# A two-block fp32 network on one core: the second block's layers without a loop, last granules in two row passes

## What is computed

```python
h = jnp.einsum('bsd,dc->bsc', x, w_in)
qa, ka, va, za, qb, kb, vb, zb, f_logit, g_logit = jnp.split(h, SPLIT_POINTS, axis=-1)
out_a = dilated_mixture(rope(qa), rope(ka), va)
up_a = jnp.einsum('bsw,wd->bsd', out_a * jax.nn.silu(za), w_up_a)
out_b = forgetting_attention(qb, kb, vb, log_f)
up_b = jnp.einsum('bsw,wd->bsd', out_b * jax.nn.silu(zb), w_up_b)
gates = jax.nn.sigmoid(g_logit + b_gate)
y = jnp.einsum('bsd,de->bse', g_a * up_a + g_b * up_b, w_out)
return layer_norm(DEEPNORM_ALPHA * x + y, ln_g, ln_b)
```

## Time and profile before

| what | value |
|---|---|
| median of 3 executions | 2982.62 us (2982.52 to 2982.68) |
| the profiled execution, its own time | 2983.63 us |
| span of the profiled execution | 2981.8 us |
| PE busy | 2835.0 us (95%) |
| DVE busy | 1838.4 us (62%) |
| ACT busy | 1352.2 us (45%) |
| DMA, 16 engines, share of the span | 58.3% for the hardware queue, 604 MB in all |
| first layer of the second block begins on PE | at 972.5 us of the span |
| first layer's last matmul ends | at 1961.2 us |
| second layer's last matmul ends | at 2964.9 us |

### The profile page before, as it was taken

One profiled execution on the slowest core, in us unless ns is written; L12 is line 12 of the kernel. 1 busy time (PEld: TensorE's weight loads), 2 busy tenths in 40 slices (PEclk: granted clock), 3 DMA queues, 4 the chain that ended last, 5 costly groups with the idle time before them and its releaser, 6 DMA issues.

```text
span 2981.8 us, 37910 instructions
## 1 busy us (share of the span) xinstructions
PE 2835.0 (95%) x13440; PEld 2346.0 (79%) x13440; DVE 1838.4 (62%) x2049; ACT 1352.2 (45%) x1741; POOL 64.0 (2%) x86
## 2 busy tenths in 40 slices
PE   1799999899999999999999999989999999999997
PEld 1578887688887788888888888868888888888886
DVE  8888988767854655555455455565655554545565
ACT  1244554444644444444454544434445445445443
POOL 0400000000000000000000000000000000000000
PEclk9899999899999999999999999989999999999999
DMA  9787678667545555556555565645554655555664
GB/s 372 279 303 267 237 249 327 215 227 231 171 142 169 192 173 171 176 198 201 188 172 173 177 190 186 228 135 176 176 177 160 229 191 176 176 177 174 194 212 141
DMA packets 165357, 604.32 MB, mean 203 GB/s; under 512 B 19192, under 2 KB 19360, under 8 KB 163904
## 3 DMA queue, kind: packets, MB, share of 16 engines
q1 hardware_dynamic: 160336, 583.08, 58.3%
q0 software_dynamic: 4848, 18.91, 2.1%
HBM read 599.79 MB, written 2.12 MB: 202 GB/s over the span
## 4 chain that ended last, share of the span: by engine, by line
PE 66%; DVE 1%; issue 1%; DMA 0%; ACT 0%; DVEq 0%; ACTq 0%; SPq 0%
PE acc L729 61%; PE psT L656 2%; PE psS L689 1%; PE psS L679 1%; PE psT L662 1%; PE psS L696 0%; DVE x L605 0%; DMA raw<-in_w 0%; DVE x L616 0%; DVE x L609 0%; ACT whi L304 0%; DVE wlo L408 0%; DVE stage L440 0%; DVE x L580 0%; DVE x L618 0%
## 5 line engine op out<-in xcount | busy, mean ns | idle before, releaser
L408 DVE TENSOR_TENSOR wlo<-raw,whi 128x1024 fp32r<-128x1024 f32 x672 | 822.7, 1225 | 863.6 <-ACT whi L304 860.5
L304 ACT ACTIVATE whi<-raw 128x1024 fp32r<-128x1024 f32 x672 | 711.6, 1060 | 991.4 <-PE acc L729 979.0
L729 PE MATMUL acc<-whi,xhi 128*128 128x512 f32 x2304 | 637.1, 398 | 9.9 <-DVE xlo L414 9.1
L729 PE MATMUL acc<-whi,xlo 128*128 128x512 f32 x2304 | 618.7, 390 | 0.0
L729 PE MATMUL acc<-wlo,xhi 128*128 128x512 f32 x2304 | 617.6, 390 | 0.0
L729 PEld LDWEIGHTS acc<-whi,xlo 128*128 128x128 f32 x2304 | 433.7, 188 | 92.5
L729 PEld LDWEIGHTS acc<-wlo,xhi 128*128 128x128 f32 x2304 | 433.0, 188 | 91.5
L729 PEld LDWEIGHTS acc<-whi,xhi 128*128 128x128 f32 x2304 | 423.5, 189 | 90.8 <-issue 9.5
L1245 ACT ACTIVATE whi<-raw 128x1024 fp32r<-128x1024 f32 x240 | 253.2, 1058 | 380.7 <-PE acc L1972 243.8
L1430 DVE TENSOR_TENSOR wlo<-raw,whi 128x1024 fp32r<-128x1024 f32 x232 | 283.0, 1223 | 163.2 <-ACT whi L1245 162.0
L1972 PE MATMUL acc<-whi,hhi 128*128 128x512 f32 x960 | 278.3, 412 | 13.6 <-DVE hlo L1441 8.3
(11 more groups left out here) (291 smaller groups left out, 1944.1 us busy)
## 6 DMA issues: line engine op xcount, KB each, us to landing
raw<-in_w SPq DMA_DIRECT2D x912, 512.0 KB, 3.5
mraw<-in_w_mod SPq DMA_DIRECT2D x150, 512.0 KB, 4.2
scr<-in_w_mod SPq DMA_DIRECT2D x31, 512.0 KB, 6.3
b_stage<-in_w_mod SPq DMA_DIRECT2D x11, 512.0 KB, 6.2
gate_row<-in_bg POOLq DMA_DIRECT2D x16, 256.0 KB, 5.2
gb<-cum_rows POOLq DMA_DIRECT2D x2, 1536.0 KB, 8.8
x<-in_x SPq DMA_DIRECT2D x1, 2048.0 KB, 8.2
gain<-in_g_post POOLq DMA_DIRECT2D x2, 1024.0 KB, 6.5
```

The lines of the kernel that those rows point to most:

```text
L304: act.activation(whi[:, n % SLOTS, :], raw[:, n % SLOTS, :], ACT.Copy).then_inc(s_hi, 1)
L408: dve.tensor_tensor(wlo[:, n % SLOTS, :], raw[:, n % SLOTS, :], whi[:, n % SLOTS, :].bitcast(F32), ALU.subtract).then_inc(s_lo, 1)
L729: m = pe.matmul(acc[c % 2][:, tb, :], a[:, kk, tile], b[:, n % SLOTS, k * CW:(k + 1) * CW], start=(kk == 0 and q == 0), stop=(kk == GK * g ...
```

## The change

**No loop.** PE, ACT and DVE have both layers written out one behind the other, and their waits compare with constants. SP's loop over the weights stays.

**The last granules** (`closing`). In the first layer the last 2 granules, in the second the last 4, run all their matmuls for row tile 0 first and then all for row tile 1. `s_half` comes at the end of row tile 0's, and `s_used` for these granules comes only in the row tile 1 pass.

**The first granules** of a layer (`leading`). The first two granules run row tile 0 for both and then row tile 1 for both. The first two fills change their shape: ("x", 0) is columns 0 to 511 of row tile 0 and ("x", 1) the same columns of row tile 1, so each holds what two granules need of one row tile.

**Between the layers** (`turn` on DVE). ACT and DVE split the next layer's first two weight granules before the residual. Then DVE carries row tile 0 through residual, statistics, deviation and the first 512 columns of the norm alone, takes up row tile 1's residual, splits fill ("x", 0), and so on. Gain and bias of columns 1024 to 2047 (`gained`) move behind the splits of granules 2 to 5 of the next layer's first chunk, in pieces of 256 columns of both row tiles.

**At the end** (`ending`). Row tile 0 is normalised while row tile 1 is still multiplied. The output goes out in five transfers by rows: 1024 and 1024 columns of row tile 0, then 1024, 512 and 512 columns of row tile 1.

The core of the diff:

```diff
+LEAD = 2
+CLOSING = (2, SLOTS)
+PIECES = ((0, 0, 2 * CW), (0, 2 * CW, 2 * CW), (1, 0, 2 * CW), (1, 2 * CW, CW), (1, 3 * CW, CW))
...
-        with act.Fori(0, DEPTH) as l:
+        for l in range(DEPTH):
...
+            if l < DEPTH - 1:
+                for g in range(LEAD):
+                    hi(g, l + 1)
+            for tb in range(TB):
+                standard_deviation(tb)
+                standardise(tb)
+                if l < DEPTH - 1:
+                    fill_hi(("x", tb), l + 1)
+            if l < DEPTH - 1:
+                hi(LEAD, l + 1)
...
+            def turn():
+
+                for g in range(LEAD):
+                    lo(g, l + 1)
+                last_residual(0)
+                variance(0)
+                inverse_deviation(0)
+                normalised(0, 0, CW).then_inc(s_xn, 1)
+                last_residual(1)
+                fill_lo(("x", 0), l + 1)
+                variance(1)
+                inverse_deviation(1)
+                normalised(1, 0, CW).then_inc(s_xn, 1)
+                link(normalised(0, CW, CW))
+                fill_lo(("x", 1), l + 1)
+                normalised(1, CW, CW).then_inc(s_xn, 2)
+                lo(LEAD, l + 1)
+
+            def ending():
+
+                last_residual(0)
+                variance(0)
+                inverse_deviation(0)
+                normalised(0, 0, 2 * CW).then_inc(s_fin, 1)
+                last_residual(1)
+                variance(1)
+                gained_rows(0, 2 * CW, 2 * CW).then_inc(s_fin, 1)
+                inverse_deviation(1)
+                normalised(1, 0, 2 * CW).then_inc(s_fin, 1)
+                gained_rows(1, 2 * CW, CW).then_inc(s_fin, 1)
+                gained_rows(1, 3 * CW, CW).then_inc(s_fin, 1)
...
+                    if c == 0 and l and g in range(LEAD, LEAD + 2 * (NCW - NV2)):
+
+                        gained(NV2 * CW + (g - LEAD) * CW // 2, CW // 2, l - 1).then_inc(s_xnp, 1)
...
+            def leading():
+
+                fill(("x", 0))
+                if l == 0:
+                    fill(("x", 1))
+                pe.wait_ge(*copied(l, ("x", 0)))
+                pe.wait_ge(s_acc[0], at(l, nch // 2, 1))
+                for g in range(LEAD):
+                    one_row(0, g, 0)
+                    if g == 0 and l:
+                        fill(("x", 1))
+                pe.wait_ge(*copied(l, ("x", 1)))
+                for g in range(LEAD):
+                    one_row(0, g, 1).then_inc(s_used, 1)
+                    if g == 0:
+                        fill(("x", 2))
+
+            def closing():
+
+                c = nch - 1
+                last = range(granules2(c) - CLOSING[l], granules2(c))
+                for tb in range(TB):
+                    for g in last:
+                        m = one_row(c, g, tb)
+                        if tb == 1:
+                            m.then_inc(s_used, 1)
+                        elif g == last[-1]:
+                            m.then_inc(s_half, 1)
```

More of the change, by code:

```diff
@@ L396, in _ @@
         links = [0]
-        with dve.Fori(0, DEPTH) as l:
+        for l in range(DEPTH):
             def link(ins):
@@ L588, in _ @@
-            link(last)
             dve.wait_ge(s_lnp, at(l, 32, 32))
             dve.memset(rtmp[:, 0:1], 0.0)
-            for tb in range(TB):
-                last = dve.bn_aggr(mv[:, tb, :], stats[:, tb, :, :])
-            last.then_inc(s_var, 1)
-            dve.wait_ge(s_std, l + 1)
-            link(dve.reciprocal(rstd[:], std[:]))
-            dve.scalar_tensor_tensor(out=nmr[:], in0=mv[:, :, 0], scalar=-1.0, in1=rstd[:], op0=ALU.mult, op1=ALU.mult)\
-                .then_inc(s_rstd, 1)
@@ L620, in _ @@
-        assert links[0] == VLINKS2, links
+            if l < DEPTH - 1:
+                turn()
+            else:
+                ending()
     @block.tensor
@@ L624, in _ @@
         pe.wait_ge(s_mem, 2)
-        with pe.Fori(0, DEPTH) as l:
+        for l in range(DEPTH):
             def fill(name):
@@ L698, in unit, with accumulate @@
                 m.then_inc(s_sfull, 1)
+            def accumulate(c, g, order):
+                ahead, alow = (ahi, alo) if CHUNKS2[c][0] == "u" else (xhi, xlo)
+                products = ((ahead, whi), (alow, whi), (ahead, wlo))
+                n = FIRST2[c] + g
+                for q, k, tb in order:
+                    a, b = products[q]
+                    kk = GK * g + k
+                    m = pe.matmul(acc[c % 2][:, tb, :], a[:, kk, tb * P:(tb + 1) * P],
+                                  b[:, n % SLOTS, k * CW:(k + 1) * CW], start=(kk == 0 and q == 0),
+                                  stop=(kk == GK * granules2(c) - 1 and q == 2))
+                return m
@@ new lines, in high, with low, one_row @@
+            def high(n):
+                pe.wait_ge(s_hi, at(l, GRAN2, n + 1))
+            def low(n):
+                pe.wait_ge(s_lo, at(l, GRAN2, n + 1))
+            def one_row(c, g, tb):
+                n = FIRST2[c] + g
+                if tb == 0:
+                    high(n)
+                accumulate(c, g, [(q, k, tb) for q in (0, 1) for k in range(GK)])
+                if tb == 0:
+                    low(n)
+                return accumulate(c, g, [(2, k, tb) for k in range(GK)])
@@ L700, in _ @@
+            def closing():
+                c = nch - 1
+                last = range(granules2(c) - CLOSING[l], granules2(c))
+                for tb in range(TB):
+                    for g in last:
[4 more added lines that the diff above has]
+                            m.then_inc(s_half, 1)
+            leading()
             for c, (kind, j) in enumerate(CHUNKS2):
-                ahead, alow = (ahi, alo) if kind == "u" else (xhi, xlo)
@@ L702, in _ @@
-                for g in range(granules2(c)):
+                for g in range(LEAD if c == 0 else 0, granules2(c) - (CLOSING[l] if c == nch - 1 else 0)):
                     for name in fills2(c, g):
@@ L716, in _ @@
                     n = FIRST2[c] + g
-                    pe.wait_ge(s_hi, at(l, GRAN2, n + 1))
-                    products = ((ahead, whi), (alow, whi), (ahead, wlo))
-                    steps = [(q, k, tb) for q in (0, 1) for k in range(GK) for tb in range(TB)]
-                    steps += [(2, k, tb) for k in range(GK) for tb in range(TB)]
-                    if n == GRAN2 - 1:
-                        steps = [(q, k, tb) for tb in range(TB) for q in range(3) for k in range(GK)]
-                    for i, (q, k, tb) in enumerate(steps):
-                        if q == 2 and all(p < 2 for p, _, _ in steps[:i]):
-                            pe.wait_ge(s_lo, at(l, GRAN2, n + 1))
-                        a, b = products[q]
-                        tile = slice(tb * P, (tb + 1) * P)
-                        kk = GK * g + k
-                        m = pe.matmul(acc[c % 2][:, tb, :], a[:, kk, tile], b[:, n % SLOTS, k * CW:(k + 1) * CW],
-                                      start=(kk == 0 and q == 0),
-                                      stop=(kk == GK * granules2(c) - 1 and q == 2))
-                        if n == GRAN2 - 1 and (q, k, tb) == (2, GK - 1, 0):
-                            m.then_inc(s_half, 1)
-                    m.then_inc(s_used, 1)
+                    high(n)
+                    accumulate(c, g, [(q, k, tb) for q in (0, 1) for k in range(GK) for tb in range(TB)])
+                    low(n)
+                    accumulate(c, g, [(2, k, tb) for k in range(GK) for tb in range(TB)]).then_inc(s_used, 1)
+            closing()
 def rope_tables():
```

157 lines of the change are left out of this document (85 added, 72 removed).

## The result

The changed kernel takes 2965.47 us (median of 6 runs, 2963.08 to 2968.32), the kernel before beside it 2982.65 us (6 runs, 2981.19 to 2984.9). The ratio is 0.9941 with a 95% interval of 0.9928 to 0.9954: faster by 17.2 us. The forecast was 2970.0 with a range of 2967.0 to 2973.0. So the direction was right, and the gain was larger than the range allowed.

What follows compares the result with a forecast made beforehand. PE, busy throughout inside the layers, was taken as the bound, leaving two seams to win: the turn between layers 8.5 us and the end 4.2, together 12.7; 2982.62 - 12.7 = 2969.9, stated as 2970.0, range 2967.0 to 2973.0.

Steps and rivals of the forecast that it cites:

- the name of a row: Between the layers: the ninth granule began at 2001.74 before, 40.6 us after the last matmul, and would begin at 1991.9.
- The clock: Behind the pause between layers: falls to half speed for about 4.4 us, net cost about 1.3 us, ends 0 and 2.5.
- Rival 1: Between the layers: the clock stays up, so the turn gives 9.8 us and the time is 2968.6; chance 0.27.
- the chosen case: Between the layers: the clock falls, the turn gives 8.5 us and the time is 2969 to 2971; chance 0.43.
- Constants in place of registers: In the waits: gives nothing, since PE is always busy; at most 0.8 us.
- The pause: Between the layers: the second layer's first product starts 3.6 to 3.8 us after the first layer's last matmul.
- The two splits ahead of the residual: End of the first layer on DVE: two more weight splits are hidden, with 0.4 us to spare.
- rival 3: Between the layers: the splits ahead of the residual wait, the turn gives only 3 to 5 us, 2974 to 2977; chance 0.06.
- rival 2: Between the layers: DVE's 3.4 us per granule against 3.21 stops PE, costing 1.5 to 3 us, 2971.5 to 2973; chance 0.12.
- rival 4: Code without a loop: PE stops at code boundaries, 1.82 us each; seven eat the 12.7, ten give 2988; chance 0.04.
- The end: After the second layer's last matmul: row tile 0 done early and a smaller last transfer give 4.2 us (3.6 to 4.3).
- Rival 5: Turn or last chain: splits overlap better or hand-overs are shorter than counted, 2965 to 2967 us; chance 0.05.

Runs made afterwards that it cites:

- e2_after_again: The changed kernel run again with no edit, against the kernel before: 2967.80 us, ratio 0.9949.
- e9_close3_warm: Changed kernel with three closing granules in the first layer, a later second weight split and 12 matmuls nobody reads between the layers: 2966.48 us.
- e5_old_end: Changed kernel with the old ending of the last layer (both row tiles through one norm, outputs by columns): 2973.20 us.

## Why the prediction was wrong in its size

**The step that failed: the name of a row.** The prediction took the product at 2001.74 in the earlier trace rows for the ninth granule's, and so had 40.6 us from the last matmul to it. It is the eighth. The row that shows it stands between those quoted (PE, kernel before):

```profile
1998.55 0.60 PE L656 MATMUL psT<-ident,x 128*128 128x128 f32 x4
...
1998.90 1.17 PE L729 MATMUL acc<-whi,xhi 128*128 128x512 f32 x4
```

1998.55 is the last of the six fills that precede the second to seventh granule. So 1998.90 is the seventh, 2001.74 the eighth and 2004.46 the ninth, and the old seam is 43.28. The forecast of the new one was counted forward from the dependences and did put the ninth granule in its place: 1991.9 less 1961.2 is 30.7 with the clock up, and 30.45 was measured where it was (e2_after_again). Old and new were taken to different granules, and the difference between them came out one warm granule, 2.72 us, too small. With this alone put right the forecast would have been 2967.3, and the rest of the miss is smaller than the range allowed.

**The clock, mis-sized.** The mechanism came as the prediction chose it: the clock was 0.50 behind the pause. Its price was set at 1.3 net (2.2 less 1.0, as written, is 1.2). Between traces of one kernel it is 0.5 with 3.4 us of the lower level and 1.1 with 6.8, and nothing where the clock stayed up. The wait in which the prediction hid 1.0 of it is there, and takes 0.90 us with the clock up. With the better count of the warm path (0.25) that is the other 1.1 us: 8.5 + 2.72 + 0.8 + 0.25 is 12.3, the seam's 12.33. Rival 1 was no rival but another outcome of the same program, as e2_after_again shows, so it was in part luck that the profiled execution showed the chosen case.

**A stop inside the layer.** Constants in place of registers were put at nothing, at most 0.8. The inner stretch came out 0.72 shorter, since PE's stop of 0.77 us at 2016.26 was absent from this trace. As the same kernel's third trace has 0.4 of it, the term is scatter at least in part; how much of it is the change stays open.

**What was right.** The pause was 3.59 for 3.6, with the chain as counted: norm, transposes, copy, split. The two splits ahead of the residual were hidden (0.34 us of wait, on PE), so rival 3 fell. From the third granule on PE set the pace, with no wait up to the ninth, so rival 2 fell. No PE stop by issue inside a layer, so rival 4 fell: PE is busy 946.92 us of 947.00 in the second layer of the changed kernel. The Trainium skill ("Runtime: NRT & Kernel Launch", section on instruction fetch) says that fetching ahead is sequential and that a taken branch breaks it; the loop's branch here cost DVE 1.82 us, and the straight line nothing that shows. Whether DVE stood there for a fetch no run here shows.

```profile
1992.00:2939.00 947.00, 946.92 (x4418) 788.45 (x4417) 510.42 (x517) 442.56 (x528) 5.38 (x10) 1.00 0.57 185
```

The end gave 4.24 for 4.2, but partly by luck, as two terms were off by 0.4 in opposite ways. DVE was done 9.66 us behind PE for the 10.1 forecast, so its chain gave 4.04 instead of 3.6; the stretch behind it, for the last transfer, shrank from 3.17 to 2.97, so the smaller transfer gave 0.2 instead of 0.6. Rival 5 described the result by its time (2965 to 2967), but not by its cause: it supposed better overlap, and 2.72 of the 3.9 missing us were there in the trace of before.

The sum with these terms put right is 12.3 + 4.2 = 16.5 for the two seams, 16.9 with the 0.7 inside and the 0.4 lost at the starts, against 17.2 measured (13.7 to 21.5 by the interval of the ratio).

## What to carry to other kernels

When a gain is the difference between a stretch counted in the old trace and one counted forward, name the same instruction at both ends, and number it by something that both programs share (here, the fills that precede each granule); one granule off was worth more than every doubtful cost in the sum. What pays at a seam between layers is to take off the path what the next matmul doesn't need, then to let its first work need only one row tile: the loop's branch was 1.3 us, gain and bias 7, the first passes by rows 4 to 5. Each of these is the price of one piece put in or taken out alone, with the clock's answer in it; together with the second closing granule's 1.2 to 1.8 they are more than the seam's 12.33, so they overlap and can't be added. Once the pause is down to a few us, compare only traces with equal time at the lower clock: 1.35 us less of pause gave 0.3 us of seam with the clock low for 6.8 us, and 0.75 with the clock up.

## What the runs showed of the hardware

The clock behind a pause of the same length isn't settled by the program. In three executions of the changed kernel, each with four transposes in a pause of 3.59 us, it stayed at 1.00, fell for 3.4 us and fell for 6.8 us, with seams of 30.45, 30.95 and 31.53. With eleven matmuls around the transposes it stayed at 1.00 in the one trace taken, and with twelve in e9_close3_warm's. Without such matmuls it fell in eight of the nine traces of the changed kernel and its variants. That the matmuls hold it is likely from this, but two traces don't show it.

Stages of unchanged code vary: over thirteen traces the first block ends between 960.47 and 967.31, and in three traces of the changed kernel the second block's first layer takes 986.20, 986.98 and 987.74. This, and not the seams, is where most of the spread of a kernel's times can lie.

A table load of ACT (1.28 us) was free or fully paid for according to its place: ahead of the wait for the variance it lies in idle time, behind it, in e5_old_end, it lay on the path.
